# Expert down weights loaded four consecutive rows to a partition, with the hidden block transposed in the same order

## The reference, cut to what matters

```
def expert_block(args):
    xb, e = args
    return (jax.nn.silu(xb @ w_gate[e]) * (xb @ w_up[e])) @ w_down[e]
```

## Time and profile before

| | |
|---|---|
| median of 3 runs | 1404.65 us (1403.72 to 1407.47) |
| the profiled execution | 1405.48 us |
| its span, first to last instruction | 1403.7 us |
| PE busy | 1262.3 us (90% of the span), 5185 matmuls |
| PEld busy | 886.2 us (63%) |
| DVE busy | 1040.5 us (74%) |
| ACT busy | 677.9 us (48%) |
| DMA packets | 78115, of them 69104 under 8 KB; 347.82 MB |
| weight loads of experts | 35 each of gate, up and down, 2048 KB each |

### The profile page before, as it was taken

One profiled execution on the slowest core, in us unless ns is written; L12 is line 12 of the kernel. 1 busy time (PEld: TensorE's weight loads), 2 busy tenths in 40 slices (PEclk: granted clock), 3 DMA queues, 4 the chain that ended last, 5 costly groups with the idle time before them and its releaser, 6 DMA issues.

```text
span 1403.7 us, 15168 instructions
## 1 busy us (share of the span) xinstructions
PE 1262.3 (90%) x5185; PEld 886.2 (63%) x5185; DVE 1040.5 (74%) x1443; ACT 677.9 (48%) x859; POOL 162.8 (12%) x169
## 2 busy tenths in 40 slices
PE   2999899949999999987999999999499999999886
PEld 2466665537777777743788854467377777777432
DVE  8678885477988888836766587856678898888253
ACT  3476401326676666613322167734276667666002
POOL 6000000010000000011000057710100000000200
PEclk9999899869999999999999999999599999999999
DMA  9637665256999999894365330022679999998641
GB/s 353 235 93 261 229 240 211 90 209 255 378 380 384 386 384 393 318 366 151 112 248 180 90 121 1 1 76 110 261 287 391 388 382 383 381 385 320 244 173 60
DMA packets 78115, 347.82 MB, mean 248 GB/s; under 512 B 12500, under 2 KB 12684, under 8 KB 69104
## 3 DMA queue, kind: packets, MB, share of 16 engines
q1 hardware_dynamic: 67184, 325.70, 61.8%
q0 software_dynamic: 7344, 16.68, 3.4%
q10 hardware_dynamic: 3536, 4.79, 0.9%
HBM read 334.15 MB, written 23.07 MB: 254 GB/s over the span
## 4 chain that ended last, share of the span: by engine, by line
PE 74%; DVE 14%; ACT 4%; DMA 4%; issue 3%; POOL 0%; SPq 0%; DVEq 0%; ACTq 0%; POOLq 0%
PE ps L1939 24%; PE ps L2062 8%; PE ps L1965 8%; PE ps L1972 6%; PE ps L1859 4%; PE ps L1930 3%; DVE scratch L1044 3%; PE ps L1866 3%; PE ps L1925 2%; PE ps L1826 2%; PE ps L2106 2%; PE ps L2134 2%; PE ps L2120 2%; DMA x_res<-in_x_dram 1%; PE ps L1821 1%
## 5 line engine op out<-in xcount | busy, mean ns | idle before, releaser
L1939 PE MATMUL ps<-slab_ring_r,gate_rows_r 128*128 128x512 f32 x512 | 201.7, 394 | 0.0
L1466 DVE TENSOR_TENSOR slab_ring_r<-slab_ring,h_t_r 128x2048 fp32r<-128x2048 f32 x64 | 143.8, 2285 | 5.6 <-ACT h_t_r L857 5.6
L2062 PE MATMUL ps<-slab_ring_r 128*128 128x512 f32 x384 | 122.1, 399 | 4.1 <-DVE h_t_r L1101 4.1
L857 ACT ACTIVATE h_t_r<-slab_ring 128x2048 fp32r<-128x2048 f32 x64 | 118.8, 1904 | 0.0
L1939 PE MATMUL ps<-h_t_r,gate_rows_r 128*128 128x512 f32 x256 | 105.6, 412 | 12.2 <-issue 7.3
L1965 PE MATMUL ps<-slab_ring,scratch 128*128 128x512 f32 x256 | 115.2, 593 | 1.5 <-ACT scratch L897 1.5
L1939 PEld LDWEIGHTS ps<-slab_ring_r,gate_rows_r 128*128 128x128 f32 x512 | 97.7, 191 | 18.6
L1939 PE MATMUL ps<-h_t_r,scratch_r 128*128 128x512 f32 x256 | 101.9, 398 | 0.0
L724 POOL TENSOR_SCALAR mod_ring<-mod_ring,row_rcp 128x512 f32<-128x512 f32 x48 | 77.0, 1617 | 206.2 <-DVE row_rcp L1712 206.2
L1466 DVE TENSOR_TENSOR slab_ring_r<-slab_ring,mod_ring_r 128x2048 fp32r<-128x2048 f32 x32 | 73.1, 2288 | 19.3 <-ACT mod_ring_r L857 19.3
L1466 DVE TENSOR_TENSOR slab_ring_r<-slab_ring,x_norm_r 128x2048 fp32r<-128x2048 f32 x32 | 73.1, 2288 | 18.3 <-ACT x_norm_r L857 18.3
(11 more groups left out here) (357 smaller groups left out, 2675.6 us busy)
## 6 DMA issues: line engine op xcount, KB each, us to landing
slab_ring<-in_expert_w_gate_dram SPq DMA_DIRECT2D x35, 2048.0 KB, 9.8
slab_ring<-in_expert_w_up_dram SPq DMA_DIRECT2D x35, 2048.0 KB, 10.0
slab_ring<-in_expert_w_down_dram SPq DMA_DIRECT2D x35, 2048.0 KB, 10.1
mod_ring<-in_mod_w_dram SPq DMA_DIRECT2D x40, 512.0 KB, 4.7
y_rows<-scratch SPq DMA_DIRECT2D x32, 512.0 KB, 10.6
slab_ring<-in_mod_w_dram SPq DMA_DIRECT2D x32, 512.0 KB, 4.6
slab_ring<-in_mod_w_dram SPq DMA_DIRECT2D x12, 1024.0 KB, 11.3
slab_ring<-in_w_qkv_dram SPq DMA_DIRECT2D x6, 2048.0 KB, 11.8
```

Source lines behind the costliest of these rows:

```text
L857: act.activation(top, w, ACT.Copy).then_inc(high_ready[c], 1)
L1466: tt_(rest, w, top.bitcast(F32), ALU.subtract).then_inc(low_ready[c], 1)
L1939: ins = pe.matmul(ps[:, bank, :], x, w, start=(kt == 0 and i == 0), stop=(kt == KT - 1 and i == 2))
L2062: ins = pe.matmul(ps[:, i % 6, :], x[:, kt, cut], y[:, k, :], start=(kt == 0 and n == 0), stop=(kt == KT - 1 and n == 2))
```

## The change

The source of a down load is cut so that partition p holds rows 4p to 4p + 3, which lie one behind the other in memory: 16 KB in one run instead of four runs of 4 KB. Slice f of the down weights in the slab is then rows f, 4 + f, 8 + f and so on. The transposes of the hidden block take every fourth column, beginning at f, so that the turned slice f has the same rows. The sums over the 512 rows are the same with their terms in another order; the rows that are split into two parts are now those of slices 0 and 1 in the new order.

```
@@ -442,7 +442,7 @@
             if c < 2:
                 return a[("expert_w_gate", "expert_w_up")[c]][l, bass.ds(e, 1)].rearrange("e (p k) n -> p (e k) n", p=P)
-            return a["expert_w_down"][l, bass.ds(e, 1)].rearrange("e (k p) n -> p (e k) n", p=P)
+            return a["expert_w_down"][l, bass.ds(e, 1)].rearrange("e (p k) n -> p (e k) n", p=P)
@@ -1941,7 +1941,7 @@
             def turn_hid(done):
                 for f in range(FT):
-                    ins = pe.transpose(ps[:, 4, f * P:(f + 1) * P], hid[:, f * P:(f + 1) * P], ident[:, :])
+                    ins = pe.transpose(ps[:, 4, f * P:(f + 1) * P], hid[:, f:HALF:FT], ident[:, :])
                 ins.then_inc(done, 1)
```

## The result

| | before | after |
|---|---|---|
| median (lowest to highest) of 7 runs each | 1404.84 us (1403.72 to 1407.47) | 1409.22 us (1408.45 to 1410.49) |
| after / before | | 1.003 [1.0018, 1.0041] |
| the profiled execution; its span | 1405.48; 1403.7 us | 1408.8; 1407.0 us |
| PE busy; PEld busy | 1262.3; 886.2 us | 1268.7; 892.2 us |
| mean granted clock | 0.950 | 0.946 |

The change makes the kernel slower by 0.3%, 4.4 us by the medians (2.5 to 5.8 by the interval). The forecast was no change, 1404.9, in a range that ended at 1408.5; the result lies just outside it.

The account below looks back on a forecast made before the run. PE, busy throughout the expert loops and holding 74% of the chain, was taken as the bound, not transfers. Terms 0.2 + 0.3 - 0.3 = +0.2 us gave 1405.7 for the profiled execution, 1404.9 us beside the runs; range 1400.7 to 1408.5.

Parts of the forecast that it names:

- The loads: Down loads in 16 KB runs land 0.2 us sooner (bounds 0.1 and 0.3), hidden behind PE in the expert loops.
- The gathers: Token-row gathers stay hidden in the loop; only layer 1's first gather, 7.53 us, is on the chain.
- cover of 27 us: In the loop, a gather issued at 455.89 is read two turns later, at 490.5, so its delay stays hidden.
- the 0.3 us that I credited: First gather of layer 1: 0.3 us off, for two down loads queued ahead, each 0.1 to 0.2 us shorter.
- rival 2: Start of layer 1's experts: wait behind four times longer runs grows fourfold, gather lands 12.6 us later; 1417.2 us; chance 0.04.
- The transposes in the loop: Strided loads run under the preceding matmul in the expert loops: 0.005 us an expert, 0.2 us on 32.
- The exposed transposes: Two layer ends and three overflow blocks, PE idle beforehand: five loads at 54 ns, 0.3 us on the path.
- The layer ends: Two of the five places without a matmul to hide the strided load, each priced at one load of 54 ns.
- Rival 1: Each of 4 x 35 hidden-block transposes pays the stride in full, 54 ns on PE: 7.6 us, 1412.2; chance 0.06.
- 18.44 named as right and the 18.6 named as wrong: Expert-loop turns still 18.44 us apart would confirm the forecast; 18.6 us or more would show the stride paid in full.
- rival 3: Transfers pace the expert loops after all: up to 0.3 us back per expert, 9.6 in all, 1395.1 us; chance 0.06.
- rival 4: Down loads are still cut into 4 KB pieces, leaving only the transposes, 0.5 us: 1405.2 us; chance 0.02.

Follow-up runs that it names:

- e1: Kernel before with only the load changed to 16 KB runs, transposes still of neighbouring columns: 1405.27 us, ratio 1.0005 [0.9996, 1.0014].
- e2: Kernel before with only the transposes of line 1944 changed to every fourth column, loads as before: 1407.80 us, ratio 1.0022 [1.0013, 1.0031].
- s2: Changed kernel with 8 KB runs instead of 16 KB and transposes reading every second column: 1406.69 us, ratio 1.0019 [1.0009, 1.0029].
- e3: Changed kernel with neighbouring columns transposed in the last expert of each layer alone: 1406.82 us, ratio 1.0018 [1.0009, 1.0026].
- r2: Changed kernel with seven unused PE matmuls around the last hidden-block transposes of each layer: 1407.08 us, ratio 1.0015 [1.0006, 1.0024].
- r3: Kernel before with seven unused PE matmuls around the last hidden-block transposes of each layer: 1405.11 us, ratio 1.0004 [0.9994, 1.0013].
- u1: Changed kernel with 24 unused PE matmuls a layer, in four pauses: 1400.86 us, ratio 0.9968 [0.9954, 0.9982].
- u2: Kernel before with 24 unused PE matmuls a layer, in four pauses, a repeat run: 1398.42 us, ratio 0.9955 [0.9942, 0.9969].

## Why the prediction was wrong

**The loads: right.** They cost nothing and bring nothing (e1: 1.0005 [0.9996, 1.0014]). 13,440 packets fewer, down loads at 9.8 us like the gate loads of before, and no transfer among the loop's waits: the table of waits of the changed kernel, 343 to 601 us, again has 12 rows, with POOL's wait for PE at their head, 202.6 instead of 200.5 us.

**The gathers: right, for a reason half right.** In the loop they land later (line 676: median 8.4 us, at most 11.9, against 7.4 and 8.1; e1 has 8.2 and e2 7.4, so it goes with the loads), far inside the cover of 27 us. The first gather of layer 1 takes 7.37 instead of 7.53 us; the 0.3 us that I credited were 0.16, which can be scatter, for e2 has 7.82 with the old loads. The rule of the Trainium skill on this ("DMA: Bandwidth & Descriptors", section "Queues, rings and completion order"), by which an engine drains some 9 to 17 descriptors of one ring before it turns to the next, would have let that gather's wait grow with the run. The trace does not agree there: it took 0.16 us less behind runs four times as long. The loop's gathers did slow, by 1.0 us, far from the fourfold of rival 2.

**The transposes in the loop: right in kind, too small.** The sum put 0.005 us on an expert, from line 1925's pace; the turns show 0.025, 0.8 us instead of 0.2 in all. The step of eight in line 1925 was the wrong neighbour: the loads of line 1944 take 210 ns, not 193, and its matmuls became 12 ns longer. The rule of the Trainium skill in "SBUF — State Buffer" (section "Door 1: The DMA port swizzle"), full rate with at least two hits in a line of 16 bytes, does not account for the loads either. By it a step of two, two floats to a line, would be at full rate. The trace does not agree: s2 measured 207 ns, the price of a step of four, against 139 for neighbours. Why line 1944 pays more than line 1925 stays open.

**The exposed transposes: two places too many, half the size.** At the layer ends the four transposes grew by 0.09 to 0.10 us, not 0.054. That the bare load was the whole price was the error: the matmul behind it grows too. And that PE sat idle before the transposes does not yet put them on the path. Of the three overflow blocks the chain has them in the second of layer 1 alone. Before:

```profile
1375.86 0.67 PE ps L1944 x4
```

After, with the first overflow block of that layer ahead of it:

```profile
1338.70 0.69 DVE scratch L1587
1339.39 1.20 DVE x_res L1604
...
1379.13 0.76 PE ps L1944 x4
```

In the first block of each layer the chain goes on with DVE's own work, and from the end of the product to line 2040 both kernels take 13.30 us in layer 0 and 12.92 in layer 1. So three places count, 0.3 us in all; the sum's 0.3 came out right because five places too cheap gave the same as three at their price, which is luck.

**The layer ends: the step that failed.** The prediction saw that at five places "there is no matmul to hide the load", and stopped there: the sum priced the longer transposes and took what follows them as unchanged, a term put at nothing without a reason. The next piece on the chain, the eight plain matmuls of line 1965, went from 3.70 to 5.40 us where the granted clock fell. Both ends together are up to 3.4 of the 4.4 us, more than all the terms that I had. As a mean it is less: at 5 falls of 8 with the step of four, two ends cost 2.1 us, and filling the pause took 2.0 off the changed kernel. The trace of before held the warning in part: PE idle before and after the transposes, in a stretch whose clock still read 1.00. It did not show how near to falling that clock was, and I had not asked what follows PE's pause, only how long the pause gets.

**The rivals.** Rival 1 (the stride paid in full, 1412.2) came nearest to the result in sign and in its cause, but not by its mechanism: the loops pay 0.025 us an expert, not 4 x 0.054. Turns of 18.48 us lie between the 18.44 named as right and the 18.6 named as wrong. Rivals 2 and 3 are excluded by the gather's 7.37 us and the table of waits, rival 4 by the packets. The mechanism that decided was on no list.

**What stays open.** What decides, in one execution, whether the clock falls at an end (6 of 10 with a step); and some 1 us that the kernels with the step take beyond what was found. Loops, three exposed places and falls are 0.8 + 0.3 + 2.1 = 3.2 of the 4.4 us; e3 lies 1 us above what was expected, r2 lies 2.0 above r3 and u1 1.7 to 2.4 above u2, where the longer transposes explain 1.1.

## What to carry to other kernels

Where PE pauses between dependent steps, price what comes after the pause, not only the pause: a tenth of a microsecond more went with 1.7 at half clock at 6 ends of 10, and filling the pause with matmuls that nobody reads cost nothing that could be told (r3: 1.0004 [0.9994, 1.0013]). A transfer that is hidden is worth nothing however much it shortens; before paying for a better layout with strided reads on the engine that sets the pace, ask who waits for the transfer. Where the effect lies in a few places that differ from execution to execution, count over several profiles before one of them is believed.

## What the hardware showed that was not expected

- A stationary load of 128 x 128 floats takes 139 ns from neighbouring columns, 207 at a step of two, 210 at a step of four, 193 at a step of eight in another buffer (line 1925): the price is not in the order of the step.
- A multiply on DVE that writes 128 x 512 floats with a step of 128 between neighbours, reading at a step of one from two sources, takes 1105 instead of 692 ns.
- A stretch of 2.33 to 2.34 us in which PE has only four transposes to do was followed by half the clock at 6 ends of 10, one of 2.24 to 2.25 us at 0 of 6.
- With unused matmuls in PE's pauses, 24 a layer, the kernel before is faster by 0.4% (0.9964 [0.9951, 0.9977], and 0.9955 [0.9942, 0.9969]); where the time was gained is shown for the end of layer 0 alone.
